# A two-layer hybrid trunk: feature-major residual, norms applied at eviction, activations stored as adjoining hi and lo tiles

## What is computed

```python
def rmsnorm(x, g):
    return x * rsqrt(mean(x * x, axis=-1) + EPS) * g

for i in range(2):
    x = x + 0.5 * swiglu(rmsnorm(x, norm_ff1[i]), ff1_w_gate[i], ff1_w_up[i], ff1_w_down[i])
    x = x + token_mixer(rmsnorm(x, norm_mix[i]), w_in[i], ...)     # w_in: 1024 x 5720
    x = x + 0.5 * swiglu(rmsnorm(x, norm_ff2[i]), ff2_w_gate[i], ff2_w_up[i], ff2_w_down[i])
    g = sigmoid(rmsnorm(x, norm_ple[i]) @ ple_w_gate[i])
    x = x + g * (p[i] @ ple_w_proj[i])
return rmsnorm(x, norm_final)
```

## Time and profile before

| | us |
|---|---|
| median of 3 runs | 1299.76 (1299.49 to 1300.05) |
| the profiled execution's own time | 1302.56 |
| its span in the trace | 1300.8 |
| TensorE busy in it | 1261.6 |
| VectorE, ScalarE, GpSimd busy | 738.2, 589.2, 92.4 |
| DMA | 223.36 MB, mean 172 GB/s |

### The profile page before, as it was taken

How to read it: one execution, slowest core, us unless ns; L and a number is a source line. 1 busy time by engine, 2 the same in 40 slices (tenths; PEclk the granted TensorE clock), 3 DMA queues, 4 the chain that set the end, 5 groups by cost and what they waited for, 6 DMA issues and landing times.

```text
span 1300.8 us, 21474 instructions
## 1 busy us (share of the span) xinstructions
PE 1261.6 (97%) x8836; PEld 1162.5 (89%) x8836; DVE 738.2 (57%) x766; ACT 589.2 (45%) x671; POOL 92.4 (7%) x120
## 2 busy tenths in 40 slices
PE   6999999999999999999999999999999999999996
PEld 6999997999988899999789999889898989999985
DVE  4545446677657554455655454557686565454464
ACT  5433444554643444334544344446455354433453
POOL 0000001002510100000000000000034100000000
PEclk9999999999999999999989999999999999999998
DMA  7655565354325365555536555644543355555541
GB/s 244 204 185 193 193 218 170 131 195 134 127 98 201 115 227 192 179 180 209 178 117 215 187 193 193 195 163 136 188 131 129 100 184 164 194 192 193 198 174 49
DMA packets 162562, 223.36 MB, mean 172 GB/s; under 512 B 10400, under 2 KB 134208, under 8 KB 162496
## 3 DMA queue, kind: packets, MB, share of 16 engines
q1 hardware_dynamic: 162496, 222.41, 51.0%
HBM read 221.35 MB, written 1.05 MB: 171 GB/s over the span
## 4 chain that ended last, share of the span: by engine, by line
PE 93%; DVE 2%; ACT 1%; issue 1%; POOL 1%; DMA 1%; SPq 0%; POOLq 0%; DVEq 0%; ACTq 0%
PE bank L375 29%; PE bank L377 29%; PE bank L376 29%; PE bank L654 2%; PE bank L431 1%; PE bank L635 1%; PE bank L540 1%; DMA raw<-in_ff_w_up 1%; POOL mean L1111 1%; PE bank L680 1%; DVE xn L1182 0%; PE bank L684 0%; PE bank L620 0%; ACT xn L824 0%; DVE x L1507 0%
## 5 line engine op out<-in xcount | busy, mean ns | idle before, releaser
L1171 DVE TENSOR_TENSOR w_lo<-raw,w_hi 128x2048 fp32r<-128x2048 f32 x204 | 471.0, 2310 | 360.0 <-ACT w_hi L812 359.9
L375 PE MATMUL bank<-h_hi,w_hi 128*128 128x256 f32 x1824 | 512.9, 281 | 2.3 <-ACT relu L890 2.3
L376 PE MATMUL bank<-h_hi,w_lo 128*128 128x256 f32 x1824 | 513.5, 282 | 0.0
L377 PE MATMUL bank<-h_lo,w_hi 128*128 128x256 f32 x1824 | 513.1, 281 | 0.0
L812 ACT ACTIVATE w_hi<-raw 128x2048 fp32r<-128x2048 f32 x204 | 389.4, 1909 | 147.5 <-PE bank L377 144.7
L375 PEld LDWEIGHTS bank<-h_hi,w_hi 128*128 128x128 f32 x1824 | 344.6, 189 | 7.5 <-issue 5.7
L377 PEld LDWEIGHTS bank<-h_lo,w_hi 128*128 128x128 f32 x1824 | 345.4, 189 | 0.0
L376 PEld LDWEIGHTS bank<-h_hi,w_lo 128*128 128x128 f32 x1824 | 342.7, 188 | 1.5
L375 PE MATMUL bank<-w_hi,small_hi 128*128 128x512 f32 x368 | 144.7, 393 | 0.0
L377 PE MATMUL bank<-w_lo,small_hi 128*128 128x512 f32 x368 | 143.9, 391 | 0.0
L376 PE MATMUL bank<-w_hi,small_lo 128*128 128x512 f32 x368 | 143.1, 389 | 0.0
(11 more groups left out here) (135 smaller groups left out, 939.9 us busy)
## 6 DMA issues: line engine op xcount, KB each, us to landing
raw<-in_ff_w_gate SPq DMA_DIRECT2D x44, 1024.0 KB, 5.0
raw<-in_ff_w_up SPq DMA_DIRECT2D x44, 1024.0 KB, 5.0
raw<-in_ff_w_down SPq DMA_DIRECT2D x44, 1024.0 KB, 4.8
raw<-in_w_in SPq DMA_DIRECT2D x44, 1024.0 KB, 4.9
raw<-in_w_out SPq DMA_DIRECT2D x8, 1024.0 KB, 4.9
raw<-in_ple_w_gate SPq DMA_DIRECT2D x8, 1024.0 KB, 4.7
raw<-in_w_branch_a SPq DMA_DIRECT2D x4, 1024.0 KB, 4.9
raw<-in_w_branch_b SPq DMA_DIRECT2D x4, 1024.0 KB, 5.0
```

The costliest lines, as they stand in the source:

```text
L375: pe.matmul(o, lh, rh, start=start, stop=False)
L376: pe.matmul(o, ll, rh, start=False, stop=False)
L377: return pe.matmul(o, lh, rl, start=False, stop=stop)
L1171: dve.tensor_tensor(w_lo[:, s, :], raw[:, s, :], w_hi[:, s, :].bitcast(F32), ALU.subtract).then_inc(lo_ready[s], 1)
```

## The change

- **Residual.** x is kept feature-major, eight tiles of 128 features x 256 tokens. All products become feature-major except the attention values and gates of w_in (av, gv, gr). The turns of x, of hidden and of p are gone. Inputs x and p, the weights (one array in the order of use) and the gains are laid out on the host, and the output is laid back there.
- **Norm.** The product takes `x * gain`, rounded (`take_pair`) and its rest (`rest_pair`), pair of tiles by pair. 1/rms of a token is formed beside it: ScalarE squares, GpSimd adds the tiles into `total`, TensorE sums over the partitions (`token_sums`), VectorE and GpSimd make 1/rms and a diagonal of it, TensorE spreads that over the partitions (`spread`), and ScalarE copies it to `rb`. Whoever empties a bank multiplies by `rb`. For attention the factor goes into the scale of the exponential and of tanh.
- **Products.** hi and lo of an activation tile lie side by side, 512 floats, and the tiles follow each other without spacing (`SKEW = 0`). Where `two` is used (gate, up, down, w_out, ple gate) one matmul moves hi and lo together against the weights' hi, and one moves hi against their lo. The bank then holds two halves, which are added at eviction. Each tile of 128 output features takes a bank of its own.
- **FFN.** All eleven gate and up chunks come first, hidden is kept whole (`hid`, 22 tiles), and eleven down chunks follow.
- **Engines.** In the FFN, ScalarE copies the low half of each bank and VectorE adds it and scales; GpSimd multiplies silu by `rb`. In the mixer VectorE, not ScalarE, empties the banks of small, gq, gk, ak and the gates.
- **Loads.** A chunk is one contiguous run of 8 KB per partition. All constants are loaded at the start.

The core of the diff:

```diff
-SKEW = 16
+SKEW = 0
+HS = 2 * T + SKEW
...
-        h_hi, h_lo = (sb(name, [P, 8, T + SKEW], F32R)[:, :, 0:T] for name in ("h_hi", "h_lo"))
+        hA = sb("hA", [P, 8, HS], F32R)
...
+            hB, hid = (over.enter_context(nc.sbuf_tensor(name, [P, n, HS], F32R)) for name, n in (("hB", 8), ("hid", 22)))
...
+            def two(o, lh, ll, hl, k, start, stop):
+                pe.matmul(o, lh, hl[:, k, 0:2 * T], start=start, stop=stop, skip_group_check=True)
+                return pe.matmul(o[:, 0:T], ll, hl[:, k, 0:T], start=False, stop=stop, skip_group_check=True)
...
+            def token_sums(L, k, b):
+                pe.wait_ge(sq_added, of_norm(L, k, 4) + START)
+                for t in range(2):
+                    mm = pe.matmul(bank[b][:, T + t:T + t + 1], total[:, t * P:(t + 1) * P], ones[:, 0:1], start=True, stop=True)
+                mm.then_inc(sums_done, 1)
+            def spread(L, k, b):
+                pe.wait_ge(diag_done, L * 4 + k + 1)
+                pe.matmul(bank[b][:, 0:T], ones[:, :], diag[:, :, :].rearrange("p a t -> p (a t)"), start=True, stop=True
+                          ).then_inc(rb_sum, 1)
...
+                pe.wait_ge(h_ready, of_norm(L, k, 4))
+                pairs(s, 0, h, 0, (6, 7))
+                token_sums(L, k, 4)
+                pairs(s, 0, h, 1, (6, 7)).then_inc(chunk_done[s], 1)
+                s = operands(L, off + 1)
+                pairs(s, 2, h, 0, range(8))
+                spread(L, k, 4)
+                pairs(s, 2, h, 1, range(8)).then_inc(chunk_done[s], 1)
+                for g in range(1, N_FF):
+                    s = operands(L, off + 2 * g)
+                    pe.wait_ge(gate_added, F + g)
+                    by_pairs(s, 0, h)
+                    s = operands(L, off + 2 * g + 1)
+                    pe.wait_ge(up_added, F + g)
+                    by_pairs(s, 2, h)
...
+            def take_pair(L, k, m, h):
+                for c in (2 * m, 2 * m + 1):
+                    dst = final[:, c, :] if h is None else h[:, c, 0:T]
+                    ins = act.activation(dst, x[:, c, :], ACT.Copy, scale=gains[:, k, c:c + 1])
+                ins.then_inc(h_hi_ready, 1)
+                act.wait_ge(sq_added, of_norm(L, k, m) + START)
+                act.activation(squared[:, :, :], x[:, 2 * m:2 * m + 2, :], ACT.Square).then_inc(sq_done, 1)
...
+                    chunk_products(L, n)
+                    act.activation(gate_low, low(0), ACT.Copy).then_inc(gate_low_ready, 1)
+                    split(L, n + 3)
...
+                    pool.wait_ge(silu_done, F + g + 1)
+                    pool.tensor_tensor(gate_act, gate_act, both(rb), ALU.mult).then_inc(silu_scaled, 1)
...
+                    dve.tensor_tensor(gate_sum, high(0), gate_low, ALU.add).then_inc(gate_added, 1)
+                    dve.tensor_tensor(gate_sum, gate_sum, both(rb), ALU.mult).then_inc(gate_scaled, 1)
+                    dve.tensor_tensor(up_sum, high(2), up_low, ALU.add).then_inc(up_added, 1)
+                    dve.tensor_tensor(gated_up, up_sum, gate_act, ALU.mult).then_inc(hidden_done, 1)
...
+            def add_half(L, m, first):
+                step(L, dve.scalar_tensor_tensor(out=xs, in0=high(first), scalar=0.5, in1=xs, op0=ALU.mult, op1=ALU.add))
+                dve.scalar_tensor_tensor(out=xs, in0=low(first), scalar=0.5, in1=xs, op0=ALU.mult, op1=ALU.add
+                                         ).then_inc(x_done, 1)
```

More of the change, by code:

```diff
@@ L349, in _ @@
-            load_x(0)
-            columns(0, 0, a["ff1_w_gate"], 0)
-            load_gain(0, 0, a["norm_ff1"][0])
-            sp.dma_start(ident, a["consts"][:, 0:P]).then_inc(const_landed, 16)
-            load_x(1)
+                for n in range(SLOTS, CHUNKS if last else CHUNKS + SLOTS):
+                    chunk(L, n)
+                    if n == FF2 + 8:
+                        sp.wait_ge(hidden_lo, L * 22 + 12)
+                        wait_stands_alone(sp, sp_ticks)
+                        sp.dma_start(p_in, a["p"][L]).then_inc(p_landed, 16)
@@ L1071, in _ @@
[L1071 removed]
+                for i in range(4):
+                    if i < 3:
+                        split(L, WOUT + 3 + i)
+                    take_pair(L, 2, i, hA)
+                split(L, WOUT + 6)
+            def embed(L, last):
+                split(L, PROJ + 3)
+                for i in range(4):
+                    n = PGATE + i
+                    chunk_products(L, n)
+                    act.activation(gate_low, low(PGATE_BANKS[i]), ACT.Copy).then_inc(pgate_low_ready, 1)
+                    if i == 0:
+                        take_rb(L, 3, 6)
+                    if i < 3 and not (last and n + 3 >= CHUNKS):
+                        split(L, n + 3)
+                    if i == 3:
+                        take_pair(L, 4, 2, None if last else hB)
+                    act.wait_ge(pgate_scaled, L * 4 + i + 1)
+                    act.activation(gate_act, gate_sum, ACT.Tanh, scale=0.5).then_inc(pgate_tanh, 1)
+                    if i in (1, 2):
+                        take_pair(L, 4, i - 1, None if last else hB)
+                take_pair(L, 4, 3, None if last else hB)
+                if not last:
+                    split(L, PGATE + 6)
@@ L1081, in layer @@
                 steps[0] = 0
-            squares(0, 0, 0)
-            split(0, 0)
-            round_h(0, 0, 0)
+            act.wait_ge(gain_landed, 16)
+            for m in range(4):
+                act.wait_ge(x_landed[m], 16)
+                take_pair(0, 0, m, hB)
+                if m == 0:
+                    split(0, 0)
             split(0, 1)
+            split(0, 2)
             with act.Fori(0, L_N - 1) as L:
```

971 lines of the change are left out of this document (433 added, 538 removed).

## The result

The changed kernel takes 1304.65 us (median of 6 runs, 1300.71 to 1305.6) against 1299.9 (6 runs, 1297.15 to 1301.05): **1.0034 times as long, 95% interval 1.0023 to 1.0045**. The forecast was 1264, range 1246 to 1296. The profiled execution of after had 1305.02 us in all.

The account below looks back on a forecast made before the run. TensorE's matmul rate plus interruptions was taken to bound the kernel. From a 1300.8 us span: stream -16.4, interruptions -24.9, start -1.6, end +7.2 give 1265.1, in all 1266.9, as a median 1264; range 1246 to 1296.

Parts of the forecast that it names:

- 2.3: Norm into the embedding, each layer: 2.3 us lost, the spread waiting under only eight pairs while a VectorE split slows GpSimd.
- P = 342: Weight products: a 512-column matmul plus a 256 takes 342 ns (340.5 + 1.7 for lost spacing); each ns is 2.37 us.
- P = 340.5: Pair time before the spacing allowance, from 512-to-256 alternations once per chunk: 227.0 and a mean of 113.5 ns.
- The upper end, 351: Slow end of the pair time's range, 336 to 351 ns, made of 231 + 120.
- Gate and up: 1408 triples of 256 columns become pairs, 354.9 to 342 ns each: -18.2 us.
- Down: Down products: 1056 matmuls of 512 become 704 pairs, -0.4 us.
- The interruptions: Stalls, transposes and half-clock time where norms interrupt TensorE's stream: 19.6 us in place of 44.5, -24.9.
- SP issues one plain load per chunk; it has no step on the path: Load queue, listed under what costs nothing: loads hold up no product, 0 us.
- The evictions of the mixer: VectorE takes over eight evictions per layer from ScalarE, in time it had idled; listed as costing nothing.
- A: Rival on the matmul stream: excess over columns is a wait for weight loads; P = 327, 36 us further, 1228; chance 0.07.
- B: Rival on activation tiles: missing spacing decides; slower from P = 357, doubled excess gives 364, +52, 1316; chance 0.12.
- C: Rival: evictions or the norm's GpSimd steps come late, and gate banks now and then; +20, 1284; chance 0.15.

Follow-up runs that it names:

- run 8: Changed kernel with VectorE, in the embedding alone, waiting for GpSimd's diagonal before its next weight splits; 1297.69 us, 0.9985 of the kernel before.
- run 10: Changed kernel with the fourth weight chunk's load issued ahead of the wait for the last norm and four small loads; 1.0041 of the kernel before.
- run 7: Changed kernel unaltered, a second profiled execution; 1303.6 us.
- run 12: TensorE alone, no trunk: 512- and 256-column matmuls in runs of 1 to 16, then other orders, halves and widths; runs of 1 took 353.2 ns a pair.
- 13: TensorE alone, no trunk: 512+256 pairs varying which half the 256 reads and writes, spacing, weights and tile; 346.7 to 353.4 ns a pair.
- run 4: Changed kernel, unspaced, with 16 floats of padding ahead of hA, so activation buffers lie 64 bytes later; 1305.98 us.

## Why the prediction was wrong

In the terms of the profiled execution the forecast was 1266.9 and after took 1305.02: 38.1 us more.

| term | forecast | measured | missed, us |
|---|---|---|---|
| pair, 2368 of them | 342 ns | 350.9 ns on the mean | 21.0 |
| embedding and way to the next layer, layer 0 | 2.3 + 4.2 | 13.5 | 7.0 |
| embedding, layer 1 | 2.3 | 6.2 | 3.9 |
| first two chunks | 4.4 | 5.3 | 0.9 |
| into mixer and into FF2, both layers | 6.4 | 5.4 | -1.0 |
| w_out, a stop at 408.15 and its like | 0 | 0.65 each | 1.3 |
| start, end | 11.5, 16.4 | 12.7, 17.1 | 1.9 |
| inside the mixers (what remains) | 0 | 3.1 | 3.1 |

**The step that failed first is P = 342**, "a 256 that follows a 512 has its successor after 110 ns ... mean 113.5" and "that gives P = 340.5". The 227.0 holds for a stream of 512s alone (226.6). Both numbers were steps between two starts at one seam per chunk, and they were taken for what a 512 and a 256 cost whenever they take turns. In the pairs of after neither came: 230.6 and 120.6 in FF1, 230.0 and 116.7 in the fastest stage. Steps of 113 behind a 512 do occur, in FF2 of layer 1 for a third of the pairs, but there the 512 ahead took 236, and another third took 241 and 120. A stream of 256s costs 120.0 each, and no run showed a pair faster than the sum with it, 346.6. The forecast had a sum of steady rates, 346.6 too, just ahead of the seam's, and left it; that the two sums agree is in part luck, since it was made of 228.3 and of the spaced 118.3. The upper end, 351 "(231 + 120)", from the unspaced rates of w_out and the branches, was the value that came.

**What follows from it.** Gate and up gained 1408 x (354.9 - 350.7) = 5.9 us instead of 18.2. Down was to give -0.4: 1056 times 228.3 ns were 241.1 us and 704 times 351.2 are 247.2, +6.1. w_out and the embedding gate got dearer by some 1.2. The mixer's threes at 119.8 were forecast right (+2.8, 1632 x (119.8 - 118.3) = 2.4). So the stream as a whole is about 4 us slower than before, where 16.4 less was forecast. With the steady rates of spaced tiles, 346.6, the forecast's own sum would have been -5.4; with the unspaced ones, 230.8 + 120.0, it would have been +4.6, about what came.

**The interruptions** fell from 44.5 to 30.4, not to 19.6. Into the mixer 0.95 (forecast 1.5), into FF2 1.8 and 1.7 (1.7): the new norm chain does what was said, and there it is hidden. In the embedding it isn't. "2.3" held the right mechanism, a split beside GpSimd's step, but charged one split and no clock: VectorE had two splits in a row, both of GpSimd's steps were slowed, and the standstill brought about six pairs at half the clock. Run 8 shows it: with the splits behind the diagonal 4.1 us go at each embedding. The window to the next layer missed a queue: "SP issues one plain load per chunk; it has no step on the path" overlooked that SyncE waits for the last tiles of h and issues four small loads (656.08 to 657.99) ahead of the fourth chunk's. That is 1.6 us (run 10). The two waits for `h_ready` there, 1.75 and 1.51, and the chain behind them were not tried apart.

**The evictions of the mixer** were to cost nothing ("before each of them it idled for ScalarE's copy of the same chunk"), and they are where the remaining 3 us point, by the trace alone. The page of after has

```profile
L348 PE MATMUL psum<-hA,w_hi 128*128 128x256 f32 x544 | 156.8, 288 | 5.4 <-DVE gates L1299 3.1
```

3.1 us of waits of the w_in products for VectorE's gates, and before 317.91 VectorE was busy with its list (`dist` alone 1.77 us) up to the gate it had to empty. In layer 0 the wait was followed by some 15 matmuls at half the clock, in layer 1, behind the same wait, by none; in run 8 both layers had them. The 4 us behind the wait, after in both layers and then run 8 in layer 1:

```profile
317.91:321.91 4.00, 4.00 (x21) 4.00 (x22) 3.45 (x7) 1.54 (x4) 0.58 (x2) 0.58 0.10 18
955.28:959.28 4.00, 4.00 (x33) 4.00 (x34) 3.45 (x7) 1.53 (x4) 0.58 (x2) 1.00 0.01 2
```

```profile
953.26:957.26 4.00, 4.00 (x22) 4.00 (x23) 3.46 (x7) 1.53 (x4) 0.57 (x2) 0.61 0.01 2
```

That is 1.4 us between two executions of the same place, nearly the 1.6 of run 10. No run moved these evictions, so their part stays argued. The 44 products of GpSimd, estimated at 1.5 each, take 2.73 and are off the path as said.

**The start and the end** were close: 12.74 against 11.5, 17.1 against 16.4.

**The rivals.** A needed 327 a pair: out. A wait for weight loads that a long matmul ahead would cover is out too, since the 512 alone carries 13.3 ns and 384 + 384 costs as much as 512 + 256 at its short period; whether the fixed part belongs to the change of weights was not tried, as every matmul in these runs loads its own. B needed 357: the spacing costs at most 2 ns a pair of the 22 that B asked for. C was right in kind, evictions and GpSimd's norm steps late, for +20; the interruptions missed by 10.8 and the mixers by 3.1, 1.6 of it by SyncE's queue and not by C. The result is P at the upper end of its range together with C. The range gave both too little room together, 1285 + 11; the worst P of the forecast plus C's 20 would have been 1305.

## To carry to other kernels

Price a new mix of instructions from steady stretches of each kind, and distrust one better number from a seam. Joining two matmuls saves a fixed cost per instruction, here some 7 of 357 ns on the mean. In this kernel, with the spacing lost, that gave gate and up 5.9 us, and down, which went from 1056 matmuls to 1408, took 6.1. Where a short step of GpSimd stands on the path, keep VectorE's long two-input instructions behind it: one wait in VectorE's list, 6 us here.

## What the runs showed that I had not expected

- **Two periods for one loop.** The unspaced pair over `hA` takes 346.7 or 353.3 ns in FF2, and with TensorE alone too. A stage keeps its level, and another execution of the same kernel has the other (run 7; between 12 and 13 one stream does it in two programs). With 16 elements of spacing gate and up stood at 349.2 in every execution and stage seen. What sets the level stays open; run length, order and halves don't. `hB` and `hid` stood at 351.2 in every unspaced execution of the whole kernel but that of run 4, where the tiles began 64 bytes later (353.3). Why they have a level of their own is open too.
- **A fixed 13.5 ns per matmul** from 256 to 512 columns, and 111.3 ns for one of 128 columns, where columns and fixed part would be 67. 512 + 128 took 339.6 ns (run 12), about 226.6 + 111.3: the 512 ahead doesn't hide it.
- **The spacing of tiles** is worth 4.8 ns a triple with other engines at work and 4.7 without, so it needs no neighbour.
